# Attention scores issued behind a pair's second branch product, sample tokens routed and gathered between the prompt's routing steps, half-wise release of the gathered copies

## What is computed

```python
def block(x, mod, lp, ctx=None):
    sh1, sc1, g1, sh2, sc2, g2 = jnp.split(mod, N_MOD, axis=-1)
    h = rmsnorm(x, lp['norm1_g']) * (1 + sc1) + sh1
    y, new = token_mixing(h, lp, ctx)
    x = x + g1 * y
    h = rmsnorm(x, lp['norm2_g']) * (1 + sc2) + sh2
    x = x + g2 * ec_moe(h, lp['w_router'], lp['w_gate'], lp['w_up'], lp['w_down'])
    return x, new

def ec_moe(h, w_router, w_gate, w_up, w_down):
    cap = CAPACITY_FACTOR * n // N_EXPERTS
    aff = jax.nn.softmax(jnp.einsum('bnd,de->ben', h, w_router).astype(jnp.float32), axis=1)
    vals, idx = lax.top_k(aff, cap)
    xg = jax.vmap(lambda hb, ib: hb[ib])(h, idx)
    ...
```

## Time and profile before

| | us |
|---|---|
| median of three runs | 1838.23 (1836.99 to 1841.49) |
| the profiled execution, its own time | 1838.3 |
| its span, first to last instruction | 1836.3 |
| PE busy | 1719.0 (94%) |
| DVE / ACT / POOL busy | 568.3 / 295.3 / 117.4 |
| loads, mean rate over the span | 291 GB/s |

### The profile page before, as it was taken

How to read it: one execution, slowest core, us unless ns; L and a number is a source line. 1 busy time by engine, 2 the same in 40 slices (tenths; PEclk the granted TensorE clock), 3 DMA queues, 4 the chain that set the end, 5 groups by cost and what they waited for, 6 DMA issues and landing times.

```text
span 1836.3 us, 18935 instructions
## 1 busy us (share of the span) xinstructions
PE 1719.0 (94%) x7216; PEld 803.3 (44%) x7216; DVE 568.3 (31%) x1245; ACT 295.3 (16%) x741; POOL 117.4 (6%) x160
## 2 busy tenths in 40 slices
PE   6998999999899988898899999999999999988987
PEld 3555555554434332242245555555544342323322
DVE  1345544352322111121124355442541221201211
ACT  2234222200200010000022333221021010100100
POOL 1151000000000000000012410000000000000000
PEclk9999999999999999999999999999999999999999
DMA  9453222354799999999993712225547999999997
GB/s 379 186 205 136 85 99 92 142 205 180 284 430 430 431 431 431 431 430 431 428 366 118 281 46 92 92 92 240 206 155 308 430 430 432 430 431 430 430 430 322
DMA packets 49104, 533.79 MB, mean 291 GB/s; under 512 B 5840, under 2 KB 6896, under 8 KB 10384
## 3 DMA queue, kind: packets, MB, share of 16 engines
q1 hardware_dynamic: 45776, 524.39, 68.3%
q0 software_dynamic: 2112, 7.97, 1.1%
q10 hardware_dynamic: 1152, 0.56, 0.1%
HBM read 530.76 MB, written 2.13 MB: 290 GB/s over the span
## 4 chain that ended last, share of the span: by engine, by line
PE 74%; DMA 21%; DVE 2%; ACT 1%; issue 1%; SPq 0%; ACTq 0%; POOL 0%; DVEq 0%; POOLq 0%
PE bank L1925 21%; DMA ring<-in_w_moe 20%; PE bank L1565 13%; PE bank L1584 7%; PE bank L1630 6%; PE bank L1962 5%; PE bank L1795 5%; PE bank L1666 2%; PE bank L1862 2%; PE bank L1731 2%; PE bank L1515 1%; PE bank L1593 1%; PE bank L1704 1%; PE bank L1608 1%; PE bank L1553 1%; PE bank L1556 1%
## 5 line engine op out<-in xcount | busy, mean ns | idle before, releaser
L1565 PE MATMUL bank<-hT,ring 128*128 128x384 f32 x768 | 259.0, 491 | 8.2 <-DVE xn L1070 4.3
L1925 PE MATMUL bank<-M,hT 128*64 128x512 f32 x1024 | 228.8, 595 | 23.6 <-DMA M<-in_w_moe 19.8
L1925 PE MATMUL bank<-ring,hT 128*64 128x512 f32 x1024 | 227.2, 595 | 11.3 <-DMA ring<-in_w_moe 11.3
L1565 PEld LDWEIGHTS bank<-hT,ring 128*128 128x128 f32 x768 | 143.2, 190 | 113.6 <-DVE xn L1070 7.9
L1925 PEld LDWEIGHTS bank<-M,hT 128*64 128x64 f32 x1024 | 72.7, 137 | 170.3 <-issue 139.3
L1925 PEld LDWEIGHTS bank<-ring,hT 128*64 128x64 f32 x1024 | 72.5, 137 | 157.9 <-issue 139.5
L1584 PE MATMUL bank<-M,ring 128*128 128x384 f32 x384 | 134.2, 492 | 4.8 <-ACT M L769 4.8
L1925 PE MATMUL bank<-ring,M 128*64 128x512 f32 x512 | 115.4, 596 | 18.6 <-DMA ring<-in_w_moe 18.6
L1925 PE MATMUL bank<-M 128*64 128x512 f32 x512 | 115.6, 595 | 12.3 <-DMA M<-in_w_moe 12.3
L1630 PE MATMUL bank<-ring,hT 128*128 128x512 f32 (+1 forms) x288 | 119.3, 574 | 1.7 <-DVE hT L1062 1.7
L962 ACT ACTIVATE hT<-bank 128x512 f32<-128x512 f32 x32 | 19.1, 597 | 574.2 <-PE bank L1925 574.2
(11 more groups left out here) (229 smaller groups left out, 1547.4 us busy)
## 6 DMA issues: line engine op xcount, KB each, us to landing
M<-in_w_moe SPq DMA_DIRECT2D x96, 2048.0 KB, 31.6
ring<-in_w_moe SPq DMA_DIRECT2D x96, 2048.0 KB, 30.6
ring<-in_w_mix SPq DMA_DIRECT2D x110, 1024.0 KB, 8.6
ring<-in_w_mix SPq DMA_DIRECT2D x4, 576.0 KB, 4.7
modrow<-in_bias_rows POOLq DMA_DIRECT2D x4, 512.0 KB, 6.7
g2slot<-in_bias_rows POOLq DMA_DIRECT2D x4, 512.0 KB, 7.6
M<-in_counts POOLq DMA_DIRECT2D x2, 768.0 KB, 12.3
out<-x SPq DMA_DIRECT2D x6, 256.0 KB, 2.0
```

The source lines that it names most:

```text
L1565: ins = mm(ps[:, 0:TOK], w[:, q, (j % 4) * P:(j % 4 + 1) * P], hT[:, 4 * h + q, :], start=(h == 0 and q == 0), stop=(h == 1 and q == 3))
L1925: ins = mm(bank[b][64 * e:64 * e + 64, :], lhs(e, 4 * h + q), w[:, q, :], start=(h == 0 and q == 0), stop=(h == 1 and q == 3))
```

## The change

It changes orders and hand-overs, and no product. In the turning stage `tq` goes behind `tkc` and `tkv`, on PE and on ACT; the banks stay. The columns of rows 6 and 7 stay between the `tkm` tiles, those of rows 8 and 9 go behind the loop's first gate product; `modcol` moves from bank 3 to bank 6, and DVE's columns and router weights go into the loop's first step. In the loop branch product 2m+1 comes ahead of the scores of m+1, and DVE merges it ahead of both maxima. In the routing the sample's four rounds of `top` run together and ahead of the prompt's x, its slots are turned ahead of the g2 rows, and the sample's gathering is laid between the prompt's last steps; ACT moves `square_x`, `normal_x` and g2's copies accordingly. `xcur_ready` becomes two semaphores, one for banks 0 and 1 and one for 2 and 3, and PE's second half of each first product waits for the second alone.

```diff
@@ -154,9 +154,9 @@
...
     if t == 2:
-        use(("modcol", 1), 3)
+        use(("modcol", 1), 6)
     for h in range(2):
-        use(("tkm", t, h), (3 + 2 * t + h) % 8 if t < 3 else 1 + h)
+        use(("tkm", t, h), ((3, 4), (5, 0), (7, 4), (1, 2))[t][h])
 for m in range(NM):
...
@@ -176,10 +176,10 @@
...
 for name, b in ((("wo", 0, 1), 5), (("wo", 1, 1), 6), (("wo", 0, 2), 7), (("xt", 1, 0), 0), (("xt", 1, 1), 1),
-                (("wo", 1, 2), 5), (("rpart", 1), 2), (("wo", 0, 0), 6), (("xt", 2, 0), 0), (("xt", 2, 1), 1),
-                (("route", 1), 3), (("rpart", 2), 2), (("wo", 1, 0), 7), (("route", 2), 3), (("xt", 0, 0), 5),
-                (("afft", 0), 4), (("modb", 10, 0), 6), (("xt", 0, 1), 5), (("modb", 11, 0), 7), (("rpart", 0), 4),
-                (("route", 0), 6), (("slt", 0), 5), (("afft", 1), 6), (("slt", 1), 7)):
+                (("wo", 1, 2), 5), (("rpart", 1), 2), (("xt", 2, 0), 0), (("route", 1), 3), (("wo", 0, 0), 6),
+                (("xt", 2, 1), 1), (("rpart", 2), 2), (("route", 2), 3), (("wo", 1, 0), 7), (("afft", 0), 4),
+                (("xt", 0, 0), 5), (("slt", 0), 4), (("modb", 10, 0), 6), (("xt", 0, 1), 5), (("modb", 11, 0), 7),
+                (("rpart", 0), 4), (("route", 0), 5), (("afft", 1), 5), (("slt", 1), 5)):
     use(name, b)
...
@@ -340,7 +340,7 @@
...
 yaT = view(18048, 4, TOK)
-wsh = view(12800, 2, KB, NE)
+wsh = view(17536, 2, KB, NE)
...
@@ -434,7 +434,8 @@
...
 vsel_ready = sem("vsel_ready")
-xcur_ready = sem("xcur_ready")
+xcur_front = sem("xcur_front")
+xcur_back = sem("xcur_back")
 th_ready = sem("th_ready")
...
@@ -819,9 +820,6 @@
...
 for t in range(T):
-    ps = wait_full(act, l, ("tq", t))
-    read(l, ("tq", t), F(qT[:, :, t * P:(t + 1) * P], ps[:, :].rearrange("p (b t) -> p b t", t=P), ACT.Copy))
-for t in range(T):
     ps = wait_full(act, l, ("tkc", t))
...
@@ -836,6 +834,9 @@
...
 read(l, ("tkv", 1), F(ckvT[:, :, 2 * P:TOK], ps[:, 0:256].rearrange("p (b t) -> p b t", t=P), ACT.Copy))
+for t in range(T):
+    ps = wait_full(act, l, ("tq", t))
+    read(l, ("tq", t), F(qT[:, :, t * P:(t + 1) * P], ps[:, :].rearrange("p (b t) -> p b t", t=P), ACT.Copy))
 mod_row(l, 7)
...
@@ -923,23 +924,25 @@
...
 turned(1, 0)
-square_x(2)
 router_part(1)
 turned(2, 0)
+square_x(2)
 expert_exp(1)
...
 normal_x(1)
+square_x(0)
 turned(0, 1)
-square_x(0)
+normal_x(2)
 router_part(0)
-normal_x(2)
-for i in (11, 10):
-    ps = wait_full(act, l, ("modb", i, 0))
-    read(l, ("modb", i, 0), F(g2slot[:, (i - 10) * 512:(i - 9) * 512], ps[:, :], ACT.Copy))
 expert_exp(0)
 normal_x(0)
+for i in (10, 11):
+    ps = wait_full(act, l, ("modb", i, 0))
+    if i == 10:
+        wait_full(act, l, ("modb", 11, 0))
+    read(l, ("modb", i, 0), F(g2slot[:, (i - 10) * 512:(i - 9) * 512], ps[:, :], ACT.Copy))
 k = 1
...
@@ -950,9 +953,9 @@
...
 F(xcur[:, kb, :, 0:CP], v[:, :, 0:CP], ACT.Identity, scale=amp[k][:, kb, 0:1],
-  bias=shift[k][:, kb, 0:1]).then_inc(xcur_ready, 1)
+  bias=shift[k][:, kb, 0:1]).then_inc(xcur_back if b > 1 else xcur_front, 1)
 F(xcur[:, kb, :, CP:USED], v[:, :, CP:USED], ACT.Identity, scale=amp[k][:, kb, 1:2],
-  bias=shift[k][:, kb, 1:2]).then_inc(xcur_ready if i == 0 else bank_read[b], 1)
+  bias=shift[k][:, kb, 1:2]).then_inc(bank_read[b] if i else xcur_back if b > 1 else xcur_front, 1)
...
@@ -1257,13 +1260,14 @@
...
     key(t)
-mod_cols(l, 1, 1, 0, KB, 3)
-for k in range(2):
-    step(V.tensor_tensor(wrA[:, k, :, :], wrout[:, :, :],
-                         amp[1][:, :, k:k + 1].to_broadcast([P, KB, 32]), ALU.mult))
-    step(V.tensor_tensor(wsh[:, k, :, :], wrout[:, :, 0:NE],
-                         shift[1][:, :, k:k + 1].to_broadcast([P, KB, NE]), ALU.mult))
-V.reduce_sum(wshift[:, :, :], wsh.rearrange("p s k e -> p s e k"), axis=AX).then_inc(wshift_ready, 1)
+def router_weights():
+
+    for k in range(2):
+        step(V.tensor_tensor(wrA[:, k, :, :], wrout[:, :, :],
+                             amp[1][:, :, k:k + 1].to_broadcast([P, KB, 32]), ALU.mult))
+        step(V.tensor_tensor(wsh[:, k, :, :], wrout[:, :, 0:NE],
+                             shift[1][:, :, k:k + 1].to_broadcast([P, KB, NE]), ALU.mult))
+    V.reduce_sum(wshift[:, :, :], wsh.rearrange("p s k e -> p s e k"), axis=AX).then_inc(wshift_ready, 1)
...
@@ -1291,16 +1295,19 @@
...
     divide(l, m, j)
+if m == 0:
+    mod_cols(l, 1, 1, 0, KB, 3)
 merge(l, m // 4, 2 * m % 8)
...
                                        ps[:, 0:TOK].rearrange("p (b t) -> p b t", t=P)))
-if m + 1 < NM:
-    maxima(l, m + 1, 0)
+    if m == 0 and j == 0:
+        router_weights()
 merge(l, m // 4, 2 * m % 8 + 1)
 if m + 1 < NM:
-    maxima(l, m + 1, 1)
+    for j in range(2):
+        maxima(l, m + 1, j)
 sum_rows(4 + m // 4, m // 2 % 2, (2 * (m % 2), 2 * (m % 2) + 1))
...
@@ -1399,23 +1406,22 @@
...
 add_mixed(1, 2)
+logits(1)
 turned(2, 1)
 x_variance(2)
-logits(1)
 affinities(1)
-add_mixed(0, 0)
 logits(2)
 affinities(2)
+add_mixed(0, 0)
+top(0, P, TOK, (0, 1, 2, 3))
+number(P, TOK)
 turned(0, 0)
-top(0, P, TOK, (0, 1))
 add_mixed(1, 0)
-top(0, P, TOK, (2, 3))
+slots(0, 1, T)
+chosen(0, (1, 2))
 x_variance(0)
-number(P, TOK)
 logits(0)
-slots(0, 1, T)
 affinities(0)
-chosen(0, (1, 2))
 top(1, 0, P, (0, 1))
...
@@ -1430,10 +1436,10 @@
...
 V.tensor_scalar(xcur[:, kb, :, 0:CP], v[:, :, 0:CP], amp[k][:, kb, 0:1], shift[k][:, kb, 0:1],
-                ALU.mult, ALU.add).then_inc(xcur_ready, 1)
+                ALU.mult, ALU.add).then_inc(xcur_back if b > 1 else xcur_front, 1)
 V.tensor_scalar(xcur[:, kb, :, CP:USED], v[:, :, CP:USED], amp[k][:, kb, 1:2],
                 shift[k][:, kb, 1:2], ALU.mult, ALU.add)\
-    .then_inc(xcur_ready if i == 0 else bank_read[b], 1)
+    .then_inc(bank_read[b] if i else xcur_back if b > 1 else xcur_front, 1)
...
@@ -1671,12 +1677,6 @@
...
 for t in range(T):
-    ps = begin(l, ("tq", t))
-    pe.wait_ge(qtok_ready, 3 * l + t + 1)
-    for b in range(4):
-        ins = turn_over(ps[:, b * P:(b + 1) * P], qtok[:, t, b * P:(b + 1) * P], ident)
-    done(l, ("tq", t), ins)
-for t in range(T):
     ps = begin(l, ("tkc", t))
...
@@ -1691,6 +1691,12 @@
...
     done(l, ("tkv", k), ins)
+for t in range(T):
+    ps = begin(l, ("tq", t))
+    pe.wait_ge(qtok_ready, 3 * l + t + 1)
+    for b in range(4):
+        ins = turn_over(ps[:, b * P:(b + 1) * P], qtok[:, t, b * P:(b + 1) * P], ident)
+    done(l, ("tq", t), ins)
 mod(l, 7)
...
@@ -1737,8 +1743,8 @@
...
 begin(l, ("modcol", 1))
-for i in range(6, 10):
-    mod_cols(l, 1, i, i - 6, i == 9)
+for i in (6, 7):
+    mod_cols(l, 1, i, i - 6, False)
 for t in (2, 3):
...
@@ -1759,15 +1765,18 @@
...
     gate(l, b, j)
-    if m not in (0, 4):
+    if m == 0:
+        for i in (8, 9):
+            mod_cols(l, 1, i, i - 6, i == 9)
+    elif m != 4:
         values(l, m - 1)
...
     turn_probs(l, m, 1)
+    branch(l, b, j + 1)
     if m + 1 < NM:
         scores(l, m + 1)
-    branch(l, b, j + 1)
 values(l, NM - 1)
...
@@ -1879,20 +1888,24 @@
...
     turn_x(1, h)
-project_out(1, 2, 0, 8)
+project_out(1, 2, 0, 4)
 router(1)
-project_out(0, 0, 0, 4)
-for h in range(2):
-    turn_x(2, h)
+turn_x(2, 0)
+project_out(1, 2, 4, 8)
 route(1)
-project_out(0, 0, 4, 8)
+project_out(0, 0, 0, 2)
+turn_x(2, 1)
+project_out(0, 0, 2, 4)
 router(2)
+project_out(0, 0, 4, 6)
+route(2)
+project_out(0, 0, 6, 8)
 project_out(1, 0, 0, 2)
-route(2)
+turn_affinities(0, 1, T)
+project_out(1, 0, 2, 5)
 turn_x(0, 0)
-project_out(1, 0, 2, 6)
-turn_affinities(0, 1, T)
-project_out(1, 0, 6, 8)
+project_out(1, 0, 5, 8)
+turn_slots(0, 1, T)
 for k in range(2):
...
@@ -1900,12 +1913,12 @@
...
 route(0)
-turn_slots(0, 1, T)
+pe.wait_ge(xn2_ready, 3 * l + 2)
+gather_sample(0, (0,))
 turn_affinities(1, 0, 1)
-pe.wait_ge(xn2_ready, 3 * l + 2)
-gather_sample(0, (0, 1, 2))
+gather_sample(0, (1,))
 turn_slots(1, 0, 1)
-gather_sample(0, (3,))
+gather_sample(0, (2, 3))
 pe.wait_ge(xn2_ready, 3 * l + 3)
...
@@ -1914,6 +1927,10 @@
...
 def project(g, b, h, lhs):
+    if c == 0 and g == 0:
+        pe.wait_ge(xcur_back if h else xcur_front, (l * NG + gr + 1) * 6)
+        for k in (2 * h, 2 * h + 1):
+            begin_pair(k, 1)
     if h == 0:
...
@@ -1961,10 +1978,6 @@
...
            start=True, stop=True).then_inc(bank_full[b], 1)
-if c == 0:
-    pe.wait_ge(xcur_ready, (l * NG + gr + 1) * 12)
-    for b in range(4):
-        begin_pair(b, 1)
 project_up(0, BANK_G[0])
...
```

## The result

The changed kernel takes 1825.15 us in the median (1824.05 to 1825.92) against 1838.59 us of the kernel before on the same chip: a ratio of 0.9921, 95% interval 0.9908 to 0.9935. 1825.2 was forecast, faster, in 1816 to 1834. One execution of cols_only took 3631.06 us at full clock and is left out of its median and ratio; nothing on record shows why.

What follows compares the result with a forecast made beforehand. Expert-weight loads bound the experts' stage, PE's order the rest, and PE's first expert product starts the loads. 3.9 - 2.5 - 4.15 - 3.8 = -6.55 us a layer, -13.1 in all, from 1838.3 to 1825.2; range 1816 to 1834.

Steps and rivals of the forecast that it cites:

- What bounds: Experts' stage: loads bound it and start with PE's first expert product; time ahead counts in full, changes inside are covered.
- Turning stage: `tq` behind `tkc` and `tkv`: bank-7 wait plus slower clock cost +3.9 us a layer (2.7 to 6.2).
- The wait: At bank 7, `mod(l, 7)` waits for ACT's last `tq` copy: begins 3.0 us later, `wq` 2.7 us later.
- The mis-sized term: Clock fall under `mod(l, 7)` and `wq` after the bank-7 wait: 0 to 3.5 us, 1.2 taken.
- the upper half: Turning stage: if transposes don't count as busy, the clock falls, giving the upper half of 2.7 to 6.2 us.
- Columns: Rows 8 and 9 and router weights moved behind the first gate product: -2.5 us a layer (-1.7 to -3.5).
- One sign: Step 0's branch product would come two to three microseconds earlier relative to the key transposes.
- Loop: Attention loop: scores cover DVE's merge, so gate products no longer wait; -4.15 us a layer.
- The new wait for tanh: Attention loop: PE idles 0.3 us before the branch product in B's steps, none in C's.
- the cold start: Attention loop: the gate product ran 0.1 slower for starting cold in its pipeline after waiting for the merge.
- The rival of a longer chain: Tanh 1.6 us later binds the loop to exponentials: +0.6 instead of -4.15, 1834.8; chance 0.15, shared with a long clock fall.
- Routing: Reordered routing and halved release bring the first expert product earlier: -3.8 us a layer (-2.7 to -4.7).

Runs made afterwards that it cites:

- cols_only: Kernel before with only the columns of rows 8 and 9, `modcol` in bank 6 and the router weights moved behind the loop's first gate product; 1830.41 us, ratio 0.9947.
- a_tq_only: Kernel before with only `tq` put behind `tkc` and `tkv` on PE and ACT; 1851.05 us, ratio 1.0058.
- one_release: Changed kernel, but PE waits for both release counts and all four banks ahead of each group's first product; 1827.73 us, ratio 0.9931.
- fill_wait: Changed kernel with three dense products that nobody reads put on PE between the last `tq` transposes and `mod(l, 7)`; 1820.76 us, ratio 0.9891.
- mod7_bank0: Changed kernel with the bank entry of `mod(l, 7)` moved from bank 7 to bank 0, `tq` still last; 1814.43 us, ratio 0.9857; again 1814.48 us.
- routing_only: Kernel before with only the routing's new order, its banks, ACT's and DVE's orders and the two release semaphores; 1831.27 us, ratio 0.9946.
- gather_12: Changed kernel with `mod(l, 7)` in bank 0 and bank 2's sample gathering moved ahead of the prompt's slot transposes; 1811.46 us, ratio 0.9846.

## Why the prediction was right, by its own steps

**What bounds.** That each us ahead of the first expert product moves the end held: experts to end is 446.2 to 446.4 us in layer 0 and 449.5 to 450.0 in layer 1 of the traces, while the first expert product itself moved between 464.2 and 483.9 us. There are two exceptions, layer 0 of a_tq_only (448.1) and layer 1 of one_release (452.9), and in both the clock was at half under the first expert products, which are what frees the slots for the stream: 48 of their records took 12.22 and 13.53 us there, against 10.52 in layer 1 of the kernel before. That nothing inside the stage counts was tried only with the release: one_release waits for both halves in every group and still takes 446.2 us in layer 0.

**Turning stage, forecast +3.9 (2.7 to 6.2).** Measured +5.7 and +4.5. The wait came out as worked: PE idles 3.12 and 3.09 us, and in fill_wait, at full clock, `mod(l, 7)` begins 3.1 us later behind `mod(l, 6)` than before and `wq` 2.7 us later, where 3.0 and 2.7 were forecast. The transposes took 3.85 us in the new order (113.14 to 116.99) and 3.50 in the old (114.43 to 117.93), not the same as the prediction has it; ACT's copies end later than either, so it costs nothing here. The mis-sized term is the clock: 1.2 taken, 2.9 and 1.7 measured. I had weighed a short fall by the earlier trace rows against a long one; in layer 0 it was the long one. The Trainium skill's sentence (TensorE: Matmul & The Clock Gate, Part 4) that transposes don't count as busy had pointed to the upper half; here the fall came behind 3.85 us of transposes, two microseconds into 3.1 us of waiting, and with three dense products in the wait it didn't come. That agrees with the page's rule but doesn't separate the transposes from the wait; and layer 1 of one_release had the same transposes and nearly the same wait without a fall, so the "surely" of the prediction was too strong.

**Columns, forecast -2.5 (-1.7 to -3.5).** Measured -3.3 and -3.1, near the end where the clock holds: 1.9 us of moved work and 1.4 us of the sixteen transposes (2.02 instead of 3.46). The other end of the range was drawn too near. With the edit in place the stretch took 45.4 us four times (layer 0 of mod7_bank0 both times and of fill_wait, layer 1 of one_release), 0.7 to 0.9 us more than before and not 1.7 less: 10.2 us ran at half clock there, where the forecast had weighed only a fall like the old one, of 3.4. One sign was badly put as well: from the start of the sixteen transposes the branch product is 1.4 us earlier and not two to three, since the moved work stood ahead of them.

**Loop, forecast -4.15.** Measured -4.1, and -4.15 alone. The steps agree too: from its first gate product to the next step's, B's step 1 went from 21.85 us (191.62 to 213.47) to 21.29 (191.95 to 213.24), and C's step 5 from 22.96 (281.35 to 304.31) to 22.13 (280.14 to 302.27): -0.56 and -0.83, where -0.55 and -0.8 were forecast. The new wait for tanh behind both exponentials was forecast at 0.3 us for B's steps and none for C's, and is 0.20 and none. In B's steps the gate product still takes 5.43 us with no idle ahead of it, so the cold start that the prediction gives as the reason for its extra 0.1 us isn't the cause there; that term and the shorter tanh wait cancel. The rival of a longer chain falls.

**Routing, forecast -3.8 (-2.7 to -4.7).** Measured -3.3 and -3.5 in this profile, where 3.4 us ran slow (16 gathering records took 3.42 us instead of 2.05), and -4.9 to -5.1 at full clock, a little past the -4.7 that the prediction gave as the most. The chain from `route(0)` was right in its parts: PE's waits are 0.90 and 1.57 us, `route(0)` begins 50.8 us after the output projection, 0.4 us sooner than worked out. Two terms were a little small: the halves of the release (1.2 taken, 1.4 found), and the 16 last gathering records with the small transpose at full clock, 2.0 us in routing_only (471.21 to 473.23) where 2.5 was taken.

**Sum.** -6.55 a layer forecast, -5.0 and -6.2 found in the profiles from mod 6 to the experts, so -11.1 us where -13.1 was worked out. The first expert product came 6.3 us earlier in layer 0, within the 6 to 7 that was named as a sign, but 1.3 of that is the start, which no step of the prediction has: the profile of before had 6.8 us at half clock there and that of the changed kernel has none. That forecast and median agree to 0.1 us is luck. In the mean of both layers the turning stage lost 1.2 us more than forecast and the routing gained 0.4 less, the columns gained 0.7 more, and the start, which the change doesn't touch, made up most of the rest. What the prediction had right are the mechanisms and the size of each part to 1.8 us a layer.

## What to carry to other kernels

When PE's order is changed, read the bank list next to it: a product that follows at once in the bank of the last transposed tile waits for the last of the other engine's copies, and one entry of the list (bank 7 to bank 0) was worth 10.7 us here, against 13.4 us for the whole change. Before a stage that is bound by a stream of loads, ask what starts the stream: here time saved ahead of it counted in full, and the earlier release of the later groups inside it not at all. And where PE waits among small products, laying real work into the wait pays: a bank of gathering took 0.9 us off each layer. In the long wait at bank 7 even products that nobody reads went with a median 4.4 us lower; in three waits of about 1 us their gain isn't shown.

## What the runs showed of the hardware that I had not expected

The granted clock moves the time of one and the same kernel by as much as some of the edits do: 1809.89 to 1816.89 us for gather_12, where the columns or the loop are worth 6 to 8 us. Places with transposes, two-column products and waits of about 1 us ran at 1.2 GHz in one profile and at 2.4 GHz in another of the same instructions, at 4.0 us for the key transposes; the start of the kernel did so too (112.6 and 112.3 us in two profiles, 111.1 to 111.7 in the others). The stretch of the key transposes, which neither edit touches, took 1.7 and 4.1 us more in a_tq_only and 2.5 and 1.8 us more in routing_only. In layer 0 of routing_only nothing ahead of it was edited either, so such a difference can't be laid on an edit from one profile. Single profiles should be compared by stretches at equal clock.
